# The last expert's second product by halves of its output, and the order of ScalarE's copies behind it

## The reference

```
h   = silu(x @ w_gate[e]) * (x @ w_up[e]) * gate[:, e]     # per expert e, 512 wide
out = sum over the chosen experts of  h @ w_down[e]        # 1024 wide
x   = layer_norm(ALPHA * x + out)
```

## Time and profile before

| | us |
|---|---|
| median of 3 runs | 3092.41 |
| lowest, highest | 3090.39, 3101.62 |
| the profiled execution | 3100.75 |
| its span, first to last instruction | 3098.9 |
| TensorE matmul busy | 2944.8 (95%) |
| VectorE busy | 2229.3 (72%) |
| ScalarE busy | 1844.7 (60%) |
| GpSimd busy | 1104.4 (36%) |

### The profile page before, as it was taken

One profiled execution on the slowest core, in us unless ns is written; L12 is line 12 of the kernel. 1 busy time (PEld: TensorE's weight loads), 2 busy tenths in 40 slices (PEclk: granted clock), 3 DMA queues, 4 the chain that ended last, 5 costly groups with the idle time before them and its releaser, 6 DMA issues.

```text
span 3098.9 us, 47519 instructions
## 1 busy us (share of the span) xinstructions
PE 2944.8 (95%) x17206; PEld 2577.5 (83%) x17206; DVE 2229.3 (72%) x4118; ACT 1844.7 (60%) x2945; POOL 1104.4 (36%) x937
## 2 busy tenths in 40 slices
PE   8889999897999997899999999999989999999998
PEld 7668888776788876699999988887779999988887
DVE  4459999435799976677666577776669666667777
ACT  4658888444688864555666555554545666555554
POOL 4520000341100004478777501002568777620000
PEclk9989999898899998899999999999999999999999
DMA  6359999541699973346666676775346666677776
GB/s 208 116 192 339 372 373 366 195 167 47 255 369 374 368 290 97 121 157 216 198 204 205 214 240 239 242 244 200 116 143 211 201 204 205 194 245 239 246 242 205
DMA packets 203994, 701.70 MB, mean 226 GB/s; under 512 B 23603, under 2 KB 24755, under 8 KB 203505
## 3 DMA queue, kind: packets, MB, share of 16 engines
q1 hardware_dynamic: 170640, 619.07, 59.1%
q10 hardware_dynamic: 21056, 40.07, 3.4%
q0 software_dynamic: 12064, 39.52, 3.3%
HBM read 659.77 MB, written 38.80 MB: 225 GB/s over the span
## 4 chain that ended last, share of the span: by engine, by line
PE 90%; DVE 5%; ACT 2%; DMA 1%; issue 1%; POOL 0%; ACTq 0%; DVEq 0%; SPq 0%
PE ps L595 89%; PE ps L606 2%; DVE hrow L105 1%; DVE arena L95 1%; DVE arena L105 1%; ACT splitb L509 1%; DVE hL L95 0%; DMA rawb<-in_peer_u 0%; DVE arena L100 0%; DMA spill<-gb 0%; POOL splitb L536 0%; ACT arena L159 0%; DMA hrow<-in_x_rows 0%; ACT hH L159 0%; DVE experts_r L95 0%
## 5 line engine op out<-in xcount | busy, mean ns | idle before, releaser
L509 ACT ACTIVATE splitb<-rawb 128x512 fp32r<-128x512 f32 (+1 forms) x1306 | 827.2, 638 | 784.8 <-PE ps L595 676.8
L536 POOL TENSOR_TENSOR splitb<-rawb,splitb 128x512 fp32r<-128x512 f32 x731 | 946.5, 1304 | 815.8 <-ACT splitb L509 803.1
L595 PE MATMUL ps<-hH,splitb 128*128 128x256 f32 x5248 | 1002.3, 287 | 5.9 <-DVE splitb L536 3.5
L595 PEld LDWEIGHTS ps<-hH,splitb 128*128 128x128 f32 x5248 | 850.2, 196 | 10.7 <-issue 5.2
L595 PE MATMUL ps<-splitb,hid 128*128 128x512 f32 x3444 | 788.8, 389 | 3.6 <-ACT hid L159 3.6
L595 PEld LDWEIGHTS ps<-splitb,hid 128*128 128x128 f32 x3444 | 646.2, 188 | 139.3 <-ACT hid L159 4.4
L595 PE MATMUL ps<-hL,splitb 128*128 128x256 f32 x2624 | 751.6, 286 | 0.0
L536 DVE TENSOR_TENSOR splitb<-rawb,splitb 128x512 fp32r<-128x512 f32 (+1 forms) x575 | 400.7, 717 | 183.4 <-ACT splitb L509 181.9
L595 PEld LDWEIGHTS ps<-hL,splitb 128*128 128x128 f32 x2624 | 513.1, 196 | 0.9 <-issue 0.5
L595 PE MATMUL ps<-experts_r 128*128 128x512 f32 (+2 forms) x1364 | 341.2, 400 | 15.8 <-ACT experts_r L159 8.6
L595 PEld LDWEIGHTS ps<-experts_r 128*128 128x128 f32 (+1 forms) x1364 | 259.1, 197 | 72.0 <-ACT experts_r L159 7.5
(11 more groups left out here) (172 smaller groups left out, 3191.9 us busy)
## 6 DMA issues: line engine op xcount, KB each, us to landing
rawb<-in_peer_u SPq DMA_DIRECT2D x256, 512.0 KB, 4.0
rawb<-in_peer_v SPq DMA_DIRECT2D x256, 512.0 KB, 4.3
experts<-in_moe_gu SPq DMA_DIRECT2D x228, 512.0 KB, 5.4
experts<-in_moe_d SPq DMA_DIRECT2D x108, 512.0 KB, 5.3
rawb<-in_moe_gu SPq DMA_DIRECT2D x92, 512.0 KB, 5.4
spill<-gb ACTq DMA_DIRECT2D x128, 256.0 KB, 4.1
aux<-spill POOLq DMA_DIRECT2D x128, 256.0 KB, 4.5
rawb<-in_moe_d SPq DMA_DIRECT2D x52, 512.0 KB, 5.4
```

What stands on the lines that cost most here:

```text
L509: self.eng.activation(S.split(m)[0], S.raw(n)[:, off:off + w], ACT.Copy).then_inc(S.hi.sem, S.hi.step(("half", m)))
L536: self.eng.tensor_tensor(l, raw, h.bitcast(F32), ALU.subtract).then_inc(self.low.sem, self.low.step(("half", m), *([("raw", n)] if last el ...
L595: return self.eng.matmul(o, w, x, start=start, stop=stop)
```

## The change

At u = 20 TensorE calls a new function, `pe_last_down`, in place of `pe_down`. It runs over the two output halves on the outside and the four weight tiles on the inside: 12 matmuls into `yb[0]`, then 12 into `yb[1]`, and names the end of each half (`moe.y`, n, i). The four tiles are released in the second run. Block 4 is then placed with the output half as the outer loop: half 0 for t = 1 and t = 0, then half 1. ScalarE at u = 20 waits for each half by itself, copies it, and calls `act.fed(4)` behind the two copies. VectorE's program is unchanged. GpSimd's and SyncE's programs are unchanged.

```diff
--- before.py
+++ after.py
@@ -1900,10 +1900,12 @@
                 self.pe_gather_over(pe)
                 yb = [pe.open("moe.y", n, i) for i in range(2)]
                 tb = [pe.open("moe.T", n, i) for i in range(2)]
+            elif u < 20:
+                self.pe_down(pe, u - 1, yb)
             else:
-                self.pe_down(pe, u - 1, yb)
-        for t in (1, 0):
-            for half in range(2):
+                self.pe_last_down(pe, u - 1, yb)
+        for half in range(2):
+            for t in (1, 0):
                 self.pe_combine_half(pe, t, half, 4)
                 S.product.at["rows", self.norm + 1, t, half] = S.product.n
 
@@ -2039,6 +2041,30 @@
             pe.out(ins, ("half", pe.half), *([("moe.down", n, u)] if j == 3 else []))
             pe.half += 1
             pe.tile += 1
+
+    def pe_last_down(self, pe, u, yb):
+
+        S, n = self.S, self.layer
+        hT, m0 = self.hT[u % 2], pe.half
+        pe.wait_ge(S.acted, "moe.hh", n, u)
+        pe.wait_ge(S.vdone, "moe.hl", n, u)
+        for i in range(2):
+            cols = slice(512 * i, 512 * i + 512)
+            for j in range(4):
+                m = m0 + j
+                hh, hl = hT[:, 128 * j:128 * j + 128], hT[:, 512 + 128 * j:640 + 128 * j]
+                pe.wait_ge(S.hi, "half", m)
+                h, l = S.split(m)
+                pe.mm(yb[i], hh, h[:, cols], False, False)
+                pe.mm(yb[i], hl, h[:, cols], False, False)
+                pe.low(m)
+                ins = pe.mm(yb[i], hh, l[:, cols], False, j == 3)
+                if i:
+                    pe.out(ins, ("half", m), *([("moe.down", n, u), ("moe.y", n, i)] if j == 3 else []))
+                elif j == 3:
+                    pe.out(ins, ("moe.y", n, i))
+        pe.half += 4
+        pe.tile += 4
 
     def pe_combine(self, pe, t, blocks):
         S, n = self.S, self.layer
@@ -2102,13 +2128,18 @@
                     act.wait_ge(S.product, "moe.pt", n, i)
                     act.cp(self.PT[:, 512 * i:512 * i + w], S.bank["moe.pt", n, i][:, 0:w], ("moe.pt", n, i),
                            ("drained", ("moe.pt", n, i)))
-            else:
+            elif u < 20:
                 act.fed(4)
                 if u % 4 == 0:
                     b = u // 4 - 1
                     act.wait_ge(S.product, "moe.down", n, u - 1)
                     for i in range(2):
                         act.cp(self.xr[:, b, 512 * i:512 * i + 512], S.bank["moe.y", n, i], ("moe.yH", n, b, i))
+            else:
+                for i in range(2):
+                    act.wait_ge(S.product, "moe.y", n, i)
+                    act.cp(self.xr[:, 4, 512 * i:512 * i + 512], S.bank["moe.y", n, i], ("moe.yH", n, 4, i))
+                act.fed(4)
 
     def act_turn(self, act, u):
         S, n = self.S, self.layer
```

## The result

| | us |
|---|---|
| changed kernel, median of 22 runs | 3090.83 (3084.93 to 3097.49) |
| kernel before, median of 22 runs | 3095.18 (3090.21 to 3103.20) |
| ratio | 0.9982, 95% interval 0.9975 to 0.9990 |
| profiled execution of the changed kernel | 3084.93, span 3083.1 |

The ratio is 5.6 us off 3095.18, with 3.1 to 7.7 inside the interval; 4.6 was forecast. It is not the quotient of the two medians, which differ by 4.35 us. What the change did must be read at its place.

What follows compares the result with a forecast made beforehand. VectorE's residual step start and later speed were taken to bound the end of each expert layer; gains of 2.32 + 2.29 = 4.6 us off 3092.41 gave 3087.8 us, range 3081 to 3096.

Steps and rivals of the forecast that it cites:

- The sum: Both expert layers together: 2.32 + 2.29 = 4.6 us off 3092.41, giving 3087.8 us.
- What bounds: End of each expert layer: VectorE's residual step start and its speed after that set the end of the stretch.
- The product by halves: Last second product: 12 matmuls in a row into one bank cost -0.1 to +0.3 us a layer, taken as 0.
- Copies first: ScalarE behind the last second product: residual step 3.40 us earlier, 2.62 from the splits, 0.78 from half 0.
- Placing by halves: TensorE after the last second product: its 3.34 us hole goes, rows come before VectorE asks for them; hidden.
- The squares: ScalarE's squares of t=1, behind the moved splits: at most 0.1 us late, hidden.
- GpSimd: GpSimd's five low halves meet VectorE's first normalising steps and take turns, giving back 1.1 us of 3.40 a layer.
- Behind the stretch: After the expert layer the rest moves as a block; GpSimd's releases come 0.6 to 1 us later, hidden.
- GpSimd free: Rival at the normalising steps: GpSimd costs nothing, gain 3.40 a layer, 6.8 us in all, 3085.6; chance 0.14.
- GpSimd at its worst: Rival: three normalising steps each lose 1.07 us to GpSimd, gain 0.4 in all, 3092.0; chance 0.08.
- One bank: Rival: 12 matmuls in a row into one bank dearer by 0.1 us each take the gain; chance 0.03.
- The clock: Rival: TensorE's clock returns later after resumptions; 9.2 us more at low clock takes the gain; chance 0.12.

Runs made afterwards that it cites:

- e3: Changed kernel, but GpSimd makes the five low halves behind each expert layer in only 8 of 512 columns; ratio to before 0.9969.
- e4: Changed kernel, first five splits each waiting only for their own buffer's last user, three of them between ScalarE's two copies; ratio to before 0.9974, repeated 0.9980.
- e1: Kernel before, with only ScalarE's copies of block 4 put ahead of the next stage's splits; ratio to before 0.9993.
- e2: Changed kernel, with ScalarE's splits ahead of the two copies again, product and placing by halves kept; ratio to before 0.9997.
- e5: e2 with block 4 placed in the old order; one run, second normalising step 10.65 us after the last second product's end.
- e6: Changed kernel with block 4 placed in the old order; one run, second normalising step 8.22 us after the last second product's end.
- e7: e4 without ScalarE's splits between its copies of the transposed rows in norms 5, 6 and 7; ratio to before 0.9961.
- e9: Changed kernel run and profiled once more, unedited; ratio to before 0.9977.
- e8: e7 with ScalarE's splits between its copies allowed again in norm 6; ratio to before 0.9969.

## Why the prediction was right

*The sum.* The gain was forecast as 4.6 us and came out as 4.9 at the marks, 5.6 (3.1 to 7.7) over the whole run. The whole run also holds what the clock does from one execution to the next, so its closeness to 4.9 is in part luck; the marks are the evidence. The 3087.8 us stood on a median of three runs, 3092.41. With 22 runs the kernel before has 3095.18, and so the changed kernel lies 3.0 us above the forecast although its gain isn't smaller.

*What bounds.* The end of the stretch was set by VectorE's start and VectorE's speed. e3 and e4 change the speed alone: the residual step stays, and N and TensorE's first matmul both come 1.12 us sooner. In e1 the residual step is 0.78 later than in the changed kernel and N 0.71. It holds only as long as the rows are placed in time; in e2 VectorE waited for TensorE.

*The product by halves.* The 40 matmuls up to T take 9.22 and 9.26 us instead of 9.21, and 9.18 in e1, which has no halves: at most 0.08 us a layer for twelve in a row into one bank, inside the -0.1 to +0.3 given.

*Copies first.* Residual step at T+1.46 and T+1.45, forecast 1.50. The split into 2.62 for the splits and 0.78 for the half was tested by e1: 2.66 and 0.78. But the halves are worth their 0.78 only behind early copies; without them they are worth nothing (e5).

*Placing by halves.* Hidden, as forecast, in the changed kernel (e6). I did not see that the same order costs 0.7 us without the early copies.

*The squares.* ScalarE's square started at T+3.25, straight behind the splits, its root was done at 572.38, and VectorE used it at 575.43: hidden.

*GpSimd.* This decided the size. Forecast: first step ending at T+4.37, second at T+6.05, N at T+8.30. Measured: 4.31, 5.98, 8.15. GpSimd's third and fourth instruction were to take 1.7 or more, and took 1.73 (571.27 to 573.00) and about 1.7 (to 574.66). The remaining 0.15 is small change: the pair ended 0.07 sooner, and the residual step of t=0 followed 0.04 instead of 0.12 behind it. The 0.77 that the prediction gives for a free step stands in none of its rows; the free ones in e7 took 0.75. Gain to N 2.47 and 2.46, forecast 2.32 and 2.29; 4.9 in all, inside the measured interval. The rule of the Trainium skill (page "SBUF — State Buffer", section "SBUF: two separate sides") holds in that the two take turns. With full times for the late one the estimate was 3.6 in all; 4.9 was measured. The late one needs less than its full time, 0.54 us for VectorE (0.75 alone) and 1.12 for GpSimd (1.27).

*Behind the stretch.* GpSimd's five low halves were to come 0.6 to 1 us later against T. The prediction's own times give 1.4 for the last (T+8.4 after T+7.04), and 1.3 was measured: hidden all the same, since the whole gain stands at TensorE's first matmul of the next stage, 2.48 us in each layer.

*The rivals.* GpSimd free: out by the pair at 2.65 and by e3 and e4, which won the missing 1.1 us a layer. GpSimd at its worst: the phase was as laid out. One bank: out. The clock: it came back sooner at the first layer and later at the second, and cost nothing over the two. It is a part of the scatter: by one-microsecond windows TensorE was busy 138 us at less than full clock in the first profile of the changed kernel and 152 us in e9, which at half speed is 7 us of the 11.4 between their spans. The rest I have not traced.

## What to carry to other kernels

Before you bring a step forward, look at what runs on the other engines at its new time: a VectorE instruction with two SBUF operands and a long GpSimd instruction hardly overlap here, and the trace showed such a meeting somewhere already, as an instruction at twice its usual length. Where an engine's list mixes work that is waited for with work that only has to be ready later, put the first ahead, and let a buffer's wait name its real last user rather than the end of the stage. Work that is moved off one chain can end up on another: in e8 nearly half of what the norms had won was lost again to splits and a transfer that now came late. A change of 0.2% has to be read at its place, against a mark such as T: there two profiles agreed within 0.01 us, while their spans differed by 11.

## What the runs showed of the hardware

In the changed kernel, a VectorE step with two SBUF inputs that met a GpSimd subtraction ended 0.54 us after it (573.00 to 573.54), and the GpSimd instruction waiting behind ended 1.12 us after VectorE (573.54 to 574.66); these were the figures of the earlier trace rows, at another place and with other tensors. A VectorE step that reads PSUM and one SBUF tensor kept its 0.69 us beside GpSimd (573.58). GpSimd instructions of 8 columns (0.20 us) left VectorE's pair at 1.54 (e3). Two runs of twelve matmuls of 512 columns, each run into one PSUM bank, cost at most 0.08 us together over the old order (9.26 against 9.18 us for 40).
